# A hybrid decoder layer with expert retrieval: one output packed, the order around the first gathers changed, the chain spread wider, the end split over partitions

## The chip, the cores and the metric

The kernel runs on one core of one Trainium2 chip. The metric is the device time of one execution in microseconds (us); the time of a kernel is the median of several runs.

## The reference, cut to what matters

A prompt of 512 rows (four tiles of 128) and 8 sample rows, all of width 1024 in fp32, go through one layer:

```python
h = x + W_out(concat[A, B, C, D](rmsnorm(x) @ W_in))     # A: causal convolution over 31 rows, B: RWKV-7, C: gated convolution over 3 rows, D: pooling
q = rmsnorm(h) @ wq                                        # 8 heads of 256 columns
s1, s2 = q[:, :, 0] . k1, q[:, :, 1] . k2                  # 128 keys each
v1, i1 = top_k(s1, 16); v2, i2 = top_k(s2, 16)
sc, pos = top_k(v1[..., :, None] + v2[..., None, :], 16)   # 16 of the 256 sums, for each head
e = i1[pos // 16] * 128 + i2[pos % 16]; g = softmax(sc)    # 128 experts a row
y = rmsnorm(h + sum_s g_s * gelu(u_tab[e_s] . h2) * v_tab[e_s])
```

`h2` is the second normalised input, rmsnorm(h). The tables u and v have 16384 rows of 1024. The new states of A to D are outputs too; C's state of the samples (`shortconv_sample`) is one of them.

## The kernel before, in words

All work is laid out by hand on five engines, each with its own instruction stream, with semaphores between them. There are two phases.

**The mixers of tiles 0 and 1.** x is normalised, turned and multiplied with the 19 column blocks of W_in, first for the band of tiles 0, 1 and the samples, then for the band of tiles 2 and 3 (`zcol` on TensorE, `zc` the copy on ScalarE, 38 in all). The weights go through three buffers, `wring`, loaded by SyncE's queue in the order of `BLOCKS` (`weights(n)` waits until a buffer is free). The mixers of the first band run between the column blocks. Then `first_out` multiplies with the eight blocks of W_out for tiles 0 and 1; three blocks of tile 1 (`ASIDE`) have buffers of their own.

**The expert slots.** `UNITS` lists 32 units, each a head and a tile, and a last one for the samples. A prompt unit has 16 slots; the samples' unit has 8, since all their heads fit in one set of 64 partitions. Slots have a running number k from 0 to 519. For each slot GpSimd issues one gather of 128 rows of 8 KB (a row of u and of v side by side) into a ring of 8 rows (`RING`); VectorE makes the dot product with u (line 1877); ScalarE makes gelu, the weight and a diagonal matrix `diag` (lines 1301 to 1307); TensorE multiplies `diag` with v into PSUM (line 1000, samples line 992) and gives the ring row free (`slot_used`). Two units ahead of its use (`LEAD`), `query` and `score` (lines 923 and 932) and VectorE's `choose` find the experts of a unit. Its weights `wqk`, 1.125 MB a head in five pieces, are loaded by SyncE's queue in `next_keys` once the previous head's last product is done. Pass 1 (units 0 to 15) takes heads 0 to 7 over tiles 0 and 1, pass 2 (units 16 to 31) heads 0 to 7 over tiles 2 and 3.

**The chain in pass 1.** The RWKV mixer of tiles 2 and 3, their output product and second norm are cut into 162 steps (`mixer(1)`, a generator on each engine). `pace(k)` says up to which step an engine goes after slot k, so the order is fixed by a formula. Step 121 (`C_OUT`) starts the output product (line 634), 162 is the last copy. `W_SLOT` is the slot from which the eight W_out blocks for it are loaded.

**Where the streams meet.** Nothing in a stream passes what is ahead of it: a DMA on SyncE's queue waits for all those issued ahead on that queue, ScalarE's `queries(2)` stands ahead of `softmax(1)`, which unit 0's last step on VectorE waits for. A change of the function table on ScalarE is an instruction of its own (ACT_TABLE_LOAD): gelu, exp, sqrt and sigmoid lie in different tables; Square and Copy need no load of their own in any row of this trace.

## Time and profile before

| | before |
|---|---|
| median of 3 runs | 1711.93 us (1711.45 to 1715.87) |
| the profiled execution, its time / its span | 1719.7 us / 1717.8 us |
| TensorE busy | 1232.3 us (72%) |
| VectorE busy | 1243.2 us (72%) |
| ScalarE busy | 700.2 us (41%) |
| GpSimd busy | 907.9 us (53%) |
| bytes moved by DMA | 606.61 MB, of them 545.29 MB by the gathers |
| granted TensorE clock, mean | 0.841 of full speed |

All rows below are of the profiled execution; their times count from the start of its span. Its own time lies 0.5% above the median of the runs. A row of the timeline gives start, duration, engine, line and operation, what is written and read, how many instructions it merges, and in brackets how long the engine was idle before it and what ended the idle time. An fp32 matmul of the source is two instructions in the trace, so "x4" for a pair of matmuls is no mistake.

### The profile page before, as it was taken

The page shows a single profiled execution, that of the slowest core. Times are in us where ns is not written, and L with a number is a line of the kernel's source. Part 1 is how long each engine was busy: PE and PEld are TensorE (multiplying, and loading weights), DVE is VectorE, ACT ScalarE, POOL GpSimd, SP SyncE. Part 2 cuts the span into 40 slices and gives each one's busy share as a digit, 9 for nine tenths or more (in the row PEclk, how much of TensorE's full clock was granted, in tenths as well). Part 3 has the DMA queues.
Part 4 walks back from the last instruction along what each step waited for, and adds up shares of the span by engine and source line. Part 5 has one row for each costly group of instructions (what it writes and reads, how often), then busy time and mean ns, then how long its engine had stood idle before and what let it go on. Part 6 is the DMA issues. An engine that isn't in the chain of part 4 may idle for free.

```text
span 1717.8 us, 19398 instructions
## 1 busy us (share of the span) xinstructions
PE 1232.3 (72%) x5360; PEld 617.3 (36%) x5360; DVE 1243.2 (72%) x2955; ACT 700.2 (41%) x1988; POOL 907.9 (53%) x1134
## 2 busy tenths in 40 slices
PE   7998888466777777769966666666666666566555
PEld 5887746222344443324322323222222322222110
DVE  3868756589788877777786777677777677767775
ACT  3322115364434444334555444343434343334344
POOL 0264012355576565545665656565656555656662
PEclk9999999677889898868997868788778788877778
DMA  6321476699999999998999999999999999999996
GB/s 199 123 86 50 95 236 178 245 401 365 386 384 417 417 417 419 417 417 362 394 414 418 419 416 418 418 415 410 414 403 416 418 410 414 404 417 417 414 408 255
DMA packets 111932, 606.61 MB, mean 353 GB/s; under 512 B 24896, under 2 KB 27456, under 8 KB 45264
## 3 DMA queue, kind: packets, MB, share of 16 engines
q0 software_dynamic: 74880, 545.29, 78.2%
q1 hardware_dynamic: 36944, 60.09, 10.8%
q8 instruction: 42, 0.69, 0.2%
q14 instruction: 66, 0.54, 0.1%
HBM read 602.15 MB, written 3.19 MB: 352 GB/s over the span
## 4 chain that ended last, share of the span: by engine, by line
DMA 39%; PE 25%; DVE 13%; POOL 7%; issue 6%; ACT 5%; DVEq 3%; SPq 2%; POOLq 0%; ACTq 0%
DMA arena<-in_uv,arena 37%; PE ps L1000 9%; DVE arena L1877 6%; PE ps L583 5%; POOL arena L2108 4%; DVEq L1340 3%; POOL arena L2107 3%; DVE arena L1343 3%; PE ps L923 3%; PE ps L647 2%; PE ps L634 2%; SPq L510 2%; DVE arena L1349 1%; ACT arena L1307 1%; PE ps L627 1%
## 5 line engine op out<-in xcount | busy, mean ns | idle before, releaser
L1000 PE MATMUL ps<-arena 128*64 128x512 f32 x2048 | 659.3, 778 | 371.9 <-ACT arena L1307 371.6
L1877 DVE CUSTOM_DVE_ANT_0 arena<-arena 128x1024 f32<-128x1024 f32 x520 | 641.6, 1235 | 301.3 <-DMA arena<-in_uv,arena 284.0
L2108 POOL DMA_INDIRECT arena<-in_uv,arena x520 | 615.4, 1184 | 88.6 <-POOL arena L2107 18.6
L2107 POOL TENSOR_TENSOR arena<-arena 1x1 f32<-1x1 f32 x520 | 210.2, 404 | 547.7 <-PE ps L1000 403.0
L1000 PEld LDWEIGHTS ps<-arena 128*64 128x64 f32 x2048 | 151.1, 164 | 753.9 <-ACT arena L1307 517.8
L1301 ACT ACTIVATE arena<-arena 128x1 f32<-128x1 f32 x520 | 105.2, 202 | 735.1 <-DVE arena L1877 733.4
L1307 ACT ACTIVATE arena<-arena 128x64 f32<-128x64 f32 (+1 forms) x520 | 181.5, 349 | 16.9
L1303 ACT ACTIVATE arena<-arena 128x1 f32<-128x1 f32 x520 | 153.2, 295 | 16.9
L1343 DVE TENSOR_TENSOR arena<-arena 128x512 f32<-128x512 f32 (+6 forms) x310 | 133.5, 431 | 30.1 <-ACT arena L1047 16.8
L923 PE MATMUL ps<-arena 128*128 128x128 f32 x1024 | 129.1, 287 | 21.6 <-DMA arena<-in_wqk 20.5
L923 PEld LDWEIGHTS ps<-arena 128*128 128x128 f32 x1024 | 123.2, 200 | 58.0 <-issue 35.7
L583 PE MATMUL ps<-arena 128*128 128x264 f32 (+1 forms) x608 | 142.6, 391 | 0.4 <-DVE arena L1343 0.4
L583 PEld LDWEIGHTS ps<-arena 128*128 128x128 f32 x608 | 116.4, 194 | 21.7 <-issue 2.5
L1928 POOL TENSOR_TENSOR arena<-arena 128x512 f32<-128x512 f32 (+12 forms) x69 | 71.1, 1038 | 99.4 <-ACT arena L1047 43.0
L647 PE MATMUL ps<-arena 128*128 128x128 f32 x576 | 80.8, 293 | 37.8 <-ACT arena L1080 25.6
L1349 DVE SCALAR_TENSOR_TENSOR arena<-arena 128x256 f32<-128x256 f32 (+4 forms) x164 | 98.1, 636 | 6.3
L647 PEld LDWEIGHTS ps<-arena 128*128 128x128 f32 x576 | 73.8, 203 | 64.2 <-issue 33.2
L1346 DVE TENSOR_SCALAR arena<-arena 64x8 f32<-64x8 f32 (+6 forms) x244 | 62.4, 260 | 25.5 <-ACT arena L1021 8.7
L1047 ACT ACTIVATE arena<-ps 128x264 f32<-128x264 f32 (+1 forms) x38 | 14.8, 388 | 114.2 <-PE ps L583 114.2
L1301 ACT ACT_TABLE_LOAD x45 | 57.7, 1283 | 0.8
L1343 DVE TENSOR_TENSOR arena<-arena,ps 128x512 f32<-128x512 f32 (+3 forms) x50 | 38.3, 793 | 22.6 <-PE ps L589 9.3
L634 PE MATMUL ps<-arena 128*128 128x512 f32 (+1 forms) x96 | 44.6, 619 | 1.6 <-DVE arena L1343 1.3
(161 smaller groups left out, 950.6 us busy)
## 6 DMA issues: line engine op xcount, KB each, us to landing
arena<-in_win SPq DMA_DIRECT2D x38, 512.0 KB, 3.3
arena<-in_wqk SPq DMA_DIRECT2D x64, 256.0 KB, 7.7
arena<-in_wout SPq DMA_DIRECT2D x24, 512.0 KB, 7.4
arena<-in_uv,arena POOLq DMA_INDIRECT x520, 12.2
arena<-in_xp SPq DMA_DIRECT2D x4, 512.0 KB, 7.2
arena<-in_wqk SPq DMA_DIRECT2D x16, 128.0 KB, 9.4
out_yp<-arena SPq DMA_DIRECT2D x4, 512.0 KB
arena<-in_const SPq DMA_DIRECT2D x1, 864.0 KB, 8.9
```

What stands on the lines that cost most here:

```text
L583: last = mm(ps[:, j % 2, 0:hi - lo], wring[:, n % 3, k, :], hT[:, k, lo:hi], start=(k == 0), stop=(k == KT - 1))
L647: last = mm(ps[:, bank, 128 * j:128 * j + 128], left[:, 4 * q + j, :], right if right is ident else right[:, 4 * q + j, :], start=True, st ...
L923: last = mm(ps[:, 4, 128 * half:128 * half + 128], wq[:, k, 128 * half:128 * half + 128], hq[t][:, k, QOFF[t]:QOFF[t] + 128], start=(k == ...
L1000: last = mm(ps[64 * q:64 * q + 64, b + c, :], diag[:, (s + q) % 8, :], ring[:, (s + q) % RING, D + 512 * c:D + 512 * c + 512], start=(s == ...
L1301: f(gl[:, b, s:s + 1], hsel[:, b, s:s + 1], ACT.Gelu).then_inc(S["gelu_done"], 1)
L1303: f(wgt[:, b, s:s + 1], gl[:, b, s:s + 1], ACT.Copy, scale=gate[:, t, s:s + 1]).then_inc(S["weight_done"], 1)
L1307: f(diag[:, s % 8, 0:64 if u < NU else NS], imask if u < NU else cst("sel2"), ACT.Copy, scale=wgt[:, b, s:s + 1]).then_inc(S["diag_done"], 1)
L1343: return v.tensor_tensor(out, i0, i1, op)
L1349: return v.scalar_tensor_tensor(out=out, in0=i0, scalar=s, in1=i1, op0=op0, op1=op1)
L1877: v.tensor_tensor_reduce(out=ring[:, s % RING, 0:D], in0=ring[:, s % RING, 0:D], in1=row, scale=1.0, scalar=0.0, op0=MUL, op1=ADD, accum_o ...
L2107: pool.tensor_tensor(carrier[:, 1:2], carrier[:, 0:1], carrier[:, 0:1], ALU.add).then_inc(S["carried"], 1)
L2108: pool.indirect_dma_start(out=ring[:, s % RING, :], out_offset=None, in_=a["uv"][:, :], in_offset=bass.IndirectOffsetOnAxis(ap=idx[:, t, s ...
```

## The change

What it does, part by part:

- **Packed state output.** The new state of C for the samples leaves from a contiguous copy `ssc_out` (made by GpSimd) instead of from a strided view of `extq`; the wait of VectorE's chain on that transfer goes.
- **Start.** x is loaded ahead of the identity; the sqrt table is loaded ahead of all else on ScalarE; tile 0's square sum, root and norm are done without waiting for tile 1 and the samples.
- **hT split.** The turned input of the two bands lies in two places, so gather 4 waits only for the first band's column blocks, and gather 5 for all.
- **First output products.** Tile 1's blocks 1 to 3 are multiplied after `score(0)`, the aside blocks are loaded later on SyncE's queue, and the steps of the convolution's layernorm for tiles 2 and 3 move behind tile 0's second norm.
- **Unit 0.** `query(2)` stands after the products of slots 0 to 5, not of 0 and 1; `queries(2)` on ScalarE at slot 7, not 5.
- **Pace.** Two chain steps in three slots instead of three in four; `W_SLOT` 166 instead of 152. The last step stands at slot 251 instead of 224.
- **Pass 2** takes heads 7 to 0, so head 7's weights are not loaded again at its start; the samples' query of a head is made beside tile 3's unit, not tile 2's.
- **Samples.** Their output product alternates between two 64-column halves of the array (one more VectorE addition); their expert products put columns 0 to 511 on partitions 0 to 7 and 512 to 1023 on 32 to 39; the final norm works on 40 x 512 instead of 8 x 1024; the sqrt table is loaded right after the last `diag`; tile 3's final norm stands 2 to 4 slots earlier; two half transfers store the result, one on ScalarE's queue.

```diff
-UNITS = [(h, t) for h in range(FIRST) for t in (0, 1)] + [(h, t) for h in range(FIRST) for t in (2, 3)] \
-    + [(h, t) for h in range(FIRST, HEADS) for t in range(TILES)]
+UNITS = [(h, t) for h in range(FIRST) for t in (0, 1)] + [(h, t) for h in reversed(range(HEADS)) for t in (2, 3)]
...
-W_SLOT = 152
+W_SLOT = 166
...
-    return 3 * (k - START) // 4
+    return 2 * (k - START) // 3
...
-            sp_.dma_start(ident, a["const"][:, 0:128]).then_inc(d_ident, 16)
             sp_.dma_start(x[:, 0, :], a["xp"][0:128, :]).then_inc(d_x[0], 16)
             sp_.dma_start(x[:, 1, :], a["xp"][128:256, :]).then_inc(d_x[1], 16)
+            sp_.dma_start(ident, a["const"][:, 0:128]).then_inc(d_ident, 16)
...
-                if n == n_out + 9:
-                    sp_.wait_ge(S["short_done"], 2)
-                    for i, j in enumerate(ASIDE):
-                        sp_.dma_start(w_aside[i], a["wout"][:, OUT_ORDER[j], :]).then_inc(d_aside, 16)
+                elif 5 <= k < 5 + len(ASIDE):
+                    if k == 5:
+                        sp_.wait_ge(S["short_done"], 2)
+                    sp_.dma_start(w_aside[k - 5], a["wout"][:, OUT_ORDER[ASIDE[k - 5]], :]).then_inc(d_aside, 16)
...
-            sp_.dma_start(a["o_ssc"][:, :, :, :], extq[:, :, :, 1:SK]).then_inc(d_ssc, 16)
+            sp_.dma_start(a["o_ssc"][:, :, :, :], ssc_out).then_inc(d_ssc, 16)
...
+            def project_samples(nh):
+                y = Y_ROWS[TILES][1]
+                for j in range(KT):
+                    p = 64 * (j % 2)
+                    last = mm(ps[p:p + NS, 5 + nh, :], y[:, OUT_ORDER[j], :], w_blocks[j][:, 512 * nh:512 * nh + 512], start=(j < 2), stop=(j >= KT - 2))
...
-            first_out(1, 0, 2)
+            first_out(1, 0, 1)
             conf_mean(1)
-            first_out(1, 2, 4)
-            conf_variance(1)
             turned(0, 0)
             turned(0, 1)
...
             query(0)
+            conf_variance(1)
             score(0)
-            first_out(1, 4, 8)
+            first_out(1, 1, 8)
...
-                if s == 0:
+                late = 4 if v == LEAD else 0
+                if s == late:
                     query(v)
-                elif s == 6:
+                elif s == (9 if late else 6):
                     score(v)
...
-                            last = mm(ps[0:NS, b + c, :], diag[:, s, 0:NS], ring[:, s % RING, D + 512 * c:D + 512 * c + 512],
+                            last = mm(ps[HALVES[c], b, :], diag[:, s, 0:NS], ring[:, s % RING, D + 512 * c:D + 512 * c + 512],
...
-            for part in (XORDER[:3], XORDER[3:]):
+            act.wait_ge(S["eps_set"], 1)
+            f(st[:, 3, 0:1], eps[:, 0:1], ACT.Sqrt)
+            for part in (XORDER[:1], XORDER[1:2], XORDER[2:3], XORDER[3:]):
...
-            final_squares(TILES)
-            final_root(TILES)
+            f(graw[:, 0:1], eps[:, 0:1], ACT.Sqrt)
+            act.wait_ge(S["unit_added"], TILES + 1)
+            f(sq2s[BOTH], xs2[BOTH], ACT.Square, accum_out=st[BOTH, 0, TILES:TILES + 1]).then_inc(S["fin_sq"], 1)
...
                     elif k == 4:
+                        pool.wait_ge(S["z_copied"], NZ)
+                    elif k == 5:
                         pool.wait_ge(S["z_copied"], len(ZORDER))
```

SyncE's queue before and after the packed output; the first row is the output of the tails, `in_lora` the small weights for the chain, `in_wqk` head 1's query weights. Before:

```order
L507 DMA out_o_tails<-arena 128x94 [waits tails_done]
L508 DMA out_o_ssc<-arena 2048x1x2
L510 DMA arena<-in_lora 128x256 [waits d_swkv]
L521 DMA arena<-in_wqk 128x512 [waits q_mm]
L521 DMA arena<-in_wqk 128x512 x3
```

After:

```order
L515 DMA out_o_tails<-arena 128x94 [waits tails_done]
L516 DMA out_o_ssc<-arena 128x32
L518 DMA arena<-in_lora 128x256 [waits d_swkv]
L529 DMA arena<-in_wqk 128x512 [waits q_mm]
L529 DMA arena<-in_wqk 128x512 x3
```

The order is the same; the state output has 128 rows of 32 values where it had 2048 pieces of 2.

TensorE from the output products of tile 1 to unit 0's slots. Before (583 is `zcol`, 589 the convolution's layernorm, 627 `first_out`, 641 `turned`, 923 and 932 query and score, 1000 the slots):

```order
L627 MATMUL ps<-arena 128x512 x4
L589 MATMUL ps<-arena 128x256 x2
L641 MATMUL ps<-arena 128x128 x8
L923 MATMUL ps<-arena 128x128 x16
L932 MATMUL ps<-arena 128x128 x2
L627 MATMUL ps<-arena 128x512 x8
L583 MATMUL ps<-arena 128x256 x32
L641 MATMUL ps<-arena 128x128 x8
L583 MATMUL ps<-arena 128x256 x8
L923 MATMUL ps<-arena 128x128 x16
L932 MATMUL ps<-arena 128x128 x2
L1000 MATMUL ps<-arena 64x512 x4
```

After (591 is `zcol`, 597 the layernorm, 635 `first_out`, 657 `turned`, 940 and 949 query and score, 1018 the slots):

```order
L597 MATMUL ps<-arena 128x256 x2
L657 MATMUL ps<-arena 128x128 x8
L940 MATMUL ps<-arena 128x128 x16
L597 MATMUL ps<-arena 128x256 x2
L949 MATMUL ps<-arena 128x128 x2
L635 MATMUL ps<-arena 128x512 x14
L591 MATMUL ps<-arena 128x256 x32
L657 MATMUL ps<-arena 128x128 x8
L591 MATMUL ps<-arena 128x256 x8
L940 MATMUL ps<-arena 128x128 x16
L949 MATMUL ps<-arena 128x128 x2
L1018 MATMUL ps<-arena 64x512 x12
```

`turned` and `query` of unit 0 have moved ahead of six matmuls of `first_out`, which now stand in one piece of 14 behind the first score; slots 0 to 5 (12 rows) stand ahead of the third query, where it was slots 0 and 1 (4 rows).

ScalarE at its end. Before (1026 is a root, 1301 to 1307 a slot's gelu, weight and diag, 1269 the final squares):

```order
L1026 ACT_TABLE_LOAD
L1026 ACTIVATE arena<-arena 128x1
L1301 ACT_TABLE_LOAD
L1301 ACTIVATE arena<-arena 128x1
L1303 ACTIVATE arena<-arena 128x1
L1307 ACTIVATE arena<-arena 128x8
L1269 ACTIVATE arena<-arena 8x1024
L1026 ACT_TABLE_LOAD
L1026 ACTIVATE arena<-arena 8x1
```

After (1320 to 1326 a slot, 1342 the table's early load, 1344 and 1346 the samples' squares and root):

```order
L1320 ACTIVATE arena<-arena 128x1
L1322 ACTIVATE arena<-arena 128x1
L1326 ACTIVATE arena<-arena 128x8
L1342 ACT_TABLE_LOAD
L1342 ACTIVATE arena<-arena 128x1
L1344 ACTIVATE arena<-arena 40x512
L1346 ACTIVATE arena<-arena 40x1
L1348 DMA out_ys<-arena 8x512
L212 UNCONDITIONAL_BRANCH
```

The root of tile 3 with its two table loads no longer stands ahead of the last slot's gelu, and the table for the samples' root is loaded ahead of the squares.

## Rows read from the trace of the kernel before

**Rows 1.** Windows: stretch, length, busy by engine, PEclk, DMA share, GB/s.

```profile
325.00:493.00 168.00, 112.14 (x476) 48.55 (x474) 134.83 (x321) 86.15 (x231) 101.01 (x124) 0.80 0.94 370
...
606.00:732.00 126.00, 95.14 (x468) 47.78 (x468) 96.22 (x245) 52.51 (x166) 72.91 (x96) 0.87 1.01 417
732.00:877.00 145.00, 119.62 (x422) 46.25 (x422) 109.02 (x259) 65.50 (x180) 77.80 (x96) 0.86 0.97 395
...
1002.00:1604.00 602.00, 401.47 (x1668) 163.53 (x1668) 431.52 (x1098) 246.50 (x776) 363.35 (x457) 0.80 1.01 413
```

**Rows 2.** SyncE's queue in time: start, us, transfer.

```profile
276.13 0.55 SPq L508 DMA_DIRECT2D out_o_ssc<-arena  x1
276.73 27.18 SPq L510 DMA_DIRECT2D arena<-in_lora  x1
303.95 9.57 SPq L521 DMA_DIRECT2D arena<-in_wqk  x4
```

**Rows 3.** DMA issues by line: count, KB each, us to landing.

```profile
arena<-in_win SPq DMA_DIRECT2D x38, 512.0 KB, 3.3
arena<-in_wqk SPq DMA_DIRECT2D x64, 256.0 KB, 7.7
...
arena<-in_uv,arena POOLq DMA_INDIRECT x520, 12.2
...
arena<-in_ssc SPq DMA_DIRECT2D x1, 16.0 KB, 3.9
out_o_ssc<-arena SPq DMA_DIRECT2D x1, 16.0 KB, 42.6
```

**Rows 4.** TensorE's timeline, 234 to 328 us.

```profile
234.68 3.66 PE L627 MATMUL ps<-arena 128*128 128x512 f32 x8
243.05 6.28 PE L627 MATMUL ps<-arena 128*128 128x512 f32 x8 [4.71 <-DMA arena<-in_wout]
...
256.41 3.81 PE L923 MATMUL ps<-arena 128*128 128x128 f32 x32 [1.04 <-DVE arena L1421]
...
287.40 3.73 PE L923 MATMUL ps<-arena 128*128 128x128 f32 x32
...
321.07 6.55 PE L923 MATMUL ps<-arena 128*128 128x128 f32 x32 [20.52 <-DMA arena<-in_wqk]
```

**Rows 5.** GpSimd's timeline, 275 to 331 us.

```profile
275.64 1.14 POOL L2108 DMA_INDIRECT arena<-in_uv,arena  x1 [0.17 <-issue]
...
329.57 0.18 POOL L2107 TENSOR_TENSOR arena<-arena 1x1 f32<-1x1 f32 x1 [25.66 <-PE ps L1000]
```

**Rows 6.** VectorE's timeline, 300 to 335 us.

```profile
305.22 1.23 DVE L1877 CUSTOM_DVE_ANT_0 arena<-arena 128x1024 f32<-128x1024 f32 x1 [1.63 <-DMA arena<-in_uv,arena]
...
331.39 0.16 DVE L1831 RECIPROCAL arena<-arena 128x1 f32<-128x1 f32 x1 [15.31 <-ACT arena L1263]
...
334.06 1.23 DVE L1877 CUSTOM_DVE_ANT_0 arena<-arena 128x1024 f32<-128x1024 f32 x1
```

**Rows 7.** Timeline at the start: ScalarE, then TensorE.

```profile
8.68 1.28 ACT L1026 ACT_TABLE_LOAD   x1
...
16.95 17.48 PE L583 MATMUL ps<-arena 128*128 128x264 f32 x64 [0.36 <-DVE arena L1343]
```

**Rows 8.** TensorE's timeline, 844 to 853 us.

```profile
844.31 7.04 PE L634 MATMUL ps<-arena 128*8 128x512 f32 x16
851.28 1.94 PE L1000 MATMUL ps<-arena 128*64 128x512 f32 x8
```

**Rows 9.** Timeline at the end: ScalarE, TensorE, VectorE.

```profile
1705.93 1.28 ACT L1301 ACT_TABLE_LOAD   x1
...
1712.48 1.28 ACT L1026 ACT_TABLE_LOAD   x1
...
1708.15 1.89 PE L992 MATMUL ps<-arena 128*8 128x512 f32 x4 [1.80 <-ACT arena L1307]
...
1714.23 1.27 DVE L1349 SCALAR_TENSOR_TENSOR arena<-arena 8x1024 f32<-8x1024 f32 x1
```

154 lines of the change are left out of this document (98 added, 56 removed).

## The prediction

> **What bounds the kernel now.** I read the windows first. From 1002 to 1604 us the DMA engines are busy throughout at 413 GB/s while TensorE and VectorE work two thirds of the time: pass 2 is the gathers' stream, and a gather of 1.049 MB costs 2.54 us there [rows 1]. Nothing that only shortens an engine's work helps in it. The same is true from 606 to 732, at 417. Two stretches move less: 325 to 493 (370 GB/s, with VectorE at 134.8 of 168 us) and 732 to 877 (395, with TensorE at 119.6 of 145) [rows 1]. At 417 GB/s they would be 168 x (1 - 370/417) = 18.9 and 145 x (1 - 395/417) = 7.6 us shorter.
>
> Then I read the queues ahead of that, because a stream that starts late ends late. TensorE stands 20.52 us ahead of the third query, waiting for head 1's `wqk` [rows 4]. SyncE's queue says why it is late: behind the state output, issued at 276.13, the small `in_lora` load occupies the queue for 27.18 us, and head 1's weights are issued only from 303.95 [rows 2]. The state output needs 42.6 us to land although it has 16 KB [rows 3]. Its 2048 pieces of 8 bytes are 128 for each of 16 DMA engines, so one piece takes 42.6/128 = 0.33 us. A gather's 8 KB row takes 8192 B over 413/16 GB/s = 0.32 us. I read it as the engines alternating between the two queues, one piece for one row. The load of the same state, also 2048 pieces, landed in 3.9 us with no gathers about [rows 3]. Meanwhile GpSimd waits 25.66 us to 329.57 for a free ring row, so the DMA engines run dry too [rows 5], and VectorE stands 15.31 us at unit 0's last choosing step, which waits for ScalarE's softmax behind `queries(2)` [rows 6].
>
> **The change part by part.**
>
> *Start, -4.* The table load at 8.68 (1.28 us) stands between the third square sum and the first root; the column blocks begin at 16.95 [rows 7]. Now the load is done before x lands, and tile 0 does not wait for two more tiles. Walking the same durations forward, the first turn starts at 7.4, the samples' is done at 12.6, the blocks start at 13.0. TensorE is near full in what follows, so 4 us stay. Bounds: 2, if the small inputs (their issue is not earlier) hold the mixer, and 4.5.
> The Trainium skill (ScalarE: Activation LUTs, What ACT_TABLE_LOAD costs) puts a table switch at 2.66 us, drain included. The row after the load here starts 1.3 us behind it, so the trace does not agree; by the page the three loads that leave the path (one here, two at the end) would give 4 us more than my sum.
>
> *Order up to the second query, -5.* TensorE idles 4.71 us at 243.05 for a W_out block that lies behind three aside blocks on the queue, the eight matmuls behind it take 6.28 instead of 3.66, and 1.04 are lost ahead of `query(0)` [rows 4]: 8.3 in sum. The asides are later now. But `turned(0)` now follows one block and waits for the second norm, about 3 us. 8.3 - 3 = 5: `query(1)` ends near 282 instead of 291.1, the start's 4 included. Bounds: 0, if the last column blocks of W_in, now loaded beside the first gathers, are late (3.3 us to land alone, a key piece beside gathers 7.7 [rows 3]), and 8.3. `score(0)` comes some 15 us earlier, so gather 0 is issued near 258 instead of 275.64 [rows 5]. I cost that at nothing: the ring holds 8 rows and the first product still waits for the last column block. The hT split likewise lets one more gather go ahead of that block; also nothing.
>
> *The queue, -15.* With 128 rows of 128 bytes there are 8 pieces an engine, and `in_lora` and the keys go at once. Head 1's weights are issued when `query(1)` is done and land in about 8 us [rows 3], before slots 0 to 5, now ahead of `query(2)`, are through. What limits then is VectorE, whose nine dot products and the choosing of unit 1 run to the dot of slot 8 as they did. So the 15.31 us go, and the 1.63 of waiting for a gather at 305.22 [rows 6]; the softmax with its table load still costs some 2. The dot of slot 9, 334.06 before, comes at 334.1 - 4 - 5 - 15 = 310. Bounds: 9, if the keys are still late by half; and more than 15, since gather 10, issued right after 329.57, could go near 294: up to 26 if VectorE did not limit.
>
> *Pace, units 0 to 3, -4.* Each slot carries 0.67 chain steps for 0.75. Of VectorE's 134.8 us, 54 dots of 1.23 and their read-out take 70 [rows 6]; choosing and chain share 65, and a ninth of the chain's part is some 3 us; waits on the chain's round trips go with it. Bounds 0 and 8.
>
> *Pace and halves, units 9 to 12, -5.* An output product holds TensorE for 7.04 us, and its samples' two are two of six [rows 8]. Spread over 10.5 slots for 9.3, with the samples' two at half, TensorE is asked for less than the gathers take. Of 7.6 us (above) I take 5; bounds 1 and 7.6. The halving is from the row behind: eight matmuls in two halves of the array take 1.94, where 16 without take 7.04, 3.5 for eight [rows 8].
> The chain now ends at slot 251 of 256. `query(16)` stands at slot 224, its input at step 143, VectorE's slot 223: just in time, at no cost, since VectorE runs a slot or two ahead of TensorE.
>
> *Head 7 kept, -2.5.* 1.18 MB at 413 GB/s are 2.9 us of a full stream; I take 2.5.
>
> *End, -4.* The load at 1705.93 ahead of the last gelu goes to an earlier slot: 1.2 [rows 9]. The one at 1712.48 is done under the last product: 1.28. Three steps over 8 x 1024 (VectorE's last of 1.27 [rows 9], its addition and ScalarE's squares, which I take as alike) become 40 x 512 and halve: 1.7. The last slot's product of 1.89 [rows 9] may halve as above: up to 0.9. Two small additions and drains cost 0.5. Between 3.7 and 4.6 in sum; I take 4, bounds 2.5 and 5.
>
> **Sum.** 4 + 5 + 15 + 4 + 5 + 2.5 + 4 = 39.5. The profiled execution, 1719.7, would be 1680.2; the median of the runs lies 7.8 below it, so 1711.9 - 39.5 = 1672.4.
>
> **The rivals.**
> *The queue stays slow.* 128-byte rows are still small, and if it is the gathers and not the pieces that hold SyncE's queue, head 1's weights are late again and only 24.5 us come back: 1687. Against it: key pieces of 2 KB rows land beside gathers in 7.7 us [rows 3].
> The Trainium skill (DMA: Bandwidth & Descriptors, Specifications) asks for at least 512 B a transfer for line rate, which 128 B does not reach; that rule speaks for this rival, and no row here has 128 B rows beside gathers.
> *The gathers alone bound it.* If VectorE is not the limit once the stop is gone, 512 gathers from 289 on at 2.54 us (1300), 14 key loads at 2.9 (40), the W_out blocks (10), some 5 to land and 9 to finish give a span of 1653, in the median near 1647; half of that way is 1659.
> *Slower.* The last W_in blocks are loaded while gathers 0 to 4 hold the DMA engines. Each block's buffer is freed by the one before it, so their delays add up. At a gather's landing of 12.2 us for 3.3 each [rows 3], five blocks would cost 44 us, more than all gains: 1716. It decides from 8.5 us late a block. Against it: only two or three are issued after gather 0, and key pieces need 7.7.
> *Nothing moves.* Only if the stop were made up later; but the stretches at 413 to 417 GB/s have no room to make up anything.
>
> **How the numbers follow.** Forecast, 1660 to 1680: 0.62. Queue stays slow, 1680 to 1692: 0.15. Towards the gathers' bound, 1647 to 1660: 0.18. Slower: 0.02; within 0.3% (about what a measurement of this kernel tells from no change): 0.01; between, 1692 to 1707: 0.02. The range 1655 to 1690 leaves 0.1 below and 0.1 above. Faster by over 0.3%: 0.97.
>
> **What would show it.** The column blocks start near 13 us. Gather 0 near 258, `query(1)` done near 282. The state output lands in under 10 us and `in_lora` holds the queue under 2. No wait over 5 us ahead of the third query, VectorE's dot of slot 9 near 310. The stretch from there to unit 4 moves near 380 GB/s, that of the output products over 405. From the start of the last product to the end under 7.5 us, for 9.65 now (1708.15 to the span's 1717.8). I am wrong if VectorE or ScalarE stands for over 10 us anywhere between 260 and 330, or if unit 16 starts with a wait for its rows.

## The result and the profile after

| | before | changed |
|---|---|---|
| median of the runs on the same chip | 1713.90 us (4 runs) | 1692.99 us (4 runs, 1692.44 to 1696.31) |
| ratio to before | | 0.9881, 95% 0.9861 to 0.9900 |
| span of the profiled execution | 1717.8 us | 1690.7 us (its own time 1692.44) |
| granted TensorE clock, mean | 0.841 | 0.847 |

The change makes the kernel faster by 20.9 us in the medians, where the forecast was 39.5. Two later measurements of the same kernel on other chips gave 0.9859 (0.9829 to 0.9889) and 0.9860 (0.9835 to 0.9885), 24.6 and 25.2 us. The two traces shown side by side differ by 27.1 us; the trace of before is one of its longer executions.

The page of the changed kernel, the row on DMA: packets, bytes, and small packets.

```profile
DMA packets 109308, 605.43 MB, mean 358 GB/s; under 512 B 22904, under 2 KB 25336, under 8 KB 42640
```

605.43 MB for 606.61: one head's keys less, as the change says.

The windows of the changed kernel, stages as in [rows 1], then two short ones at the end: stretch, length, busy by engine, PEclk, DMA share, GB/s.

```profile
306.00:467.50 161.50, 107.76 (x460) 48.15 (x460) 133.83 (x328) 87.39 (x230) 95.69 (x116) 0.79 0.97 379
704.00:862.00 158.00, 119.64 (x448) 50.07 (x450) 113.91 (x281) 63.38 (x189) 85.11 (x107) 0.85 0.98 395
816.00:862.00 46.00, 42.86 (x156) 17.73 (x154) 32.84 (x81) 20.60 (x58) 27.43 (x34) 0.96 0.89 344
978.00:1579.50 601.50, 400.86 (x1662) 166.27 (x1664) 430.31 (x1093) 247.22 (x773) 354.77 (x456) 0.80 1.01 414
1664.00:1670.00 6.00, 3.10 (x12) 0.34 (x12) 3.47 (x7) 4.06 (x10) 2.98 (x4) 0.99 1.03 430
1679.00:1686.00 7.00, 3.77 (x8) 0.22 (x8) 1.92 (x3) 3.30 (x9) 0.00 (x0) 0.50 0.01 5
```

The stretch from the third query to unit 4 moves 379 GB/s for 370 (380 was forecast). The stretch with the output products stays at 395 (over 405 was forecast), and in its last third it falls to 344, with TensorE busy in 42.86 of 46 us. Pass 2 is the same stream: 414 for 413.

The start of the changed kernel in the timeline (against [rows 7]).

```profile
13.23 1.06 ACT L1039 ACTIVATE arena<-arena 128x1024 f32<-128x1024 f32 x1 [3.97 <-DMA arena<-in_xp]
...
15.69 0.15 DVE L1370 TENSOR_SCALAR arena<-arena 128x1 f32<-128x1 f32 x1 [1.12 <-ACT arena L1039]
15.76 0.21 DVE L1367 TENSOR_TENSOR arena<-ps,arena 128x64 f32<-128x64 f32 x1
...
16.03 15.96 PE L591 MATMUL ps<-arena 128*128 128x264 f32 x64 [3.32 <-DVE arena L1367]
```

The column blocks start at 16.03, not at 13. TensorE waits 3.32 us for VectorE's step on the samples' turned rows (15.76), and VectorE has just done a mean at 15.69, of the last tile: its square sum follows the one at 13.23, which waited 3.97 us for x. The samples stand in VectorE's order behind the means of tiles 2 and 3.

SyncE's queue (against [rows 2]), and the landing of the state output (against [rows 3]).

```profile
248.47 0.43 SPq L512 DMA_DIRECT2D arena<-in_wout  x1
...
250.19 0.44 SPq L512 DMA_DIRECT2D arena<-in_wout  x1
251.54 19.81 SPq L471 DMA_DIRECT2D arena<-in_win  x4
...
271.86 0.43 SPq L516 DMA_DIRECT2D out_o_ssc<-arena  x1
272.34 0.43 SPq L518 DMA_DIRECT2D arena<-in_lora  x1
288.35 2.04 SPq L529 DMA_DIRECT2D arena<-in_wqk  x4
```

```profile
out_o_ssc<-arena SPq DMA_DIRECT2D x1, 16.0 KB, 7.3
```

The state output lands in 7.3 us, `in_lora` occupies the queue for 0.43 us where it was 27.18, and head 1's keys are issued at 288.35, 15.6 us earlier than in [rows 2].

ScalarE's last copy of a second-band column block ahead of the first score, TensorE between 251 and 310 us, and GpSimd's gathers (against [rows 4, 5]).

```profile
231.15 0.39 ACT L1067 ACTIVATE arena<-ps 128x256 f32<-128x256 f32 x1 [10.77 <-PE ps L591]
...
251.93 1.99 PE L635 MATMUL ps<-arena 128*128 128x512 f32 x4 [0.42 <-DMA arena<-in_wout]
256.94 7.12 PE L635 MATMUL ps<-arena 128*128 128x512 f32 x12 [3.02 <-DMA arena<-in_wout]
...
275.60 3.73 PE L591 MATMUL ps<-arena 128*128 128x256 f32 x16 [1.15 <-DMA arena<-in_win]
...
284.59 3.73 PE L940 MATMUL ps<-arena 128*128 128x128 f32 x32
...
306.04 3.84 PE L940 MATMUL ps<-arena 128*128 128x128 f32 x32
...
258.61 1.14 POOL L2164 DMA_INDIRECT arena<-in_uv,arena  x1 [0.17 <-issue]
...
285.25 0.18 POOL L2163 TENSOR_TENSOR arena<-arena 1x1 f32<-1x1 f32 x1 [20.04 <-ACT arena L1067]
```

The wait of 20.52 us ahead of the third query is gone. Gather 0 goes at 258.61, as forecast. But `query(1)` starts at 284.59 and ends at 288.3, not at 282. TensorE waits 0.42 and 3.02 us for `in_wout`, pays 7.12 us for twelve matmuls behind the second wait (the granted clock is 0.79 from 256 to 264 us; in a later trace, at 1.00, the twelve take 5.43), and waits 1.15 us for `in_win` at 275.60. The queue shows why. The three aside blocks are issued one at a time between the ring's blocks; the last goes at 250.19 and lands at 256.89, where TensorE's second wait ends. The row of `in_win` merges four issues of 0.33 us each, between which SyncE waits for free buffers. Two of them, at 267.55 and 271.02, go behind gathers 0 to 4 and take 8.01 and 7.72 us to land, where the last two of before took 3.15 and 3.67; TensorE's wait at 275.60 is for the first of these. GpSimd then waits 20.04 us, so the early gathers bring no early stream.

Of the two signs of being wrong that the prediction named, the first comes up at its edge: ScalarE stands 13.01 us, until 267.56, for a column block that comes behind the run of output products; 7.6 us of that lie behind 260. VectorE stands nowhere over 6 us there. The second does not come up: unit 16's first dot waits 0.20 us, and the 2.10 us that VectorE waits for `in_nf` just ahead of it fall where the DMA share is 1.01.

VectorE in the changed kernel: the softmax's reciprocal in unit 0, the dot of slot 9, and the first dots of units 4, 9 and 13 (against [rows 6]); then the latter three in the kernel before.

```profile
312.05 0.16 DVE L1856 RECIPROCAL arena<-arena 128x1 f32<-128x1 f32 x1 [0.86 <-ACT arena L1282]
...
314.75 1.23 DVE L1928 CUSTOM_DVE_ANT_0 arena<-arena 128x1024 f32<-128x1024 f32 x1
...
467.49 1.23 DVE L1928 CUSTOM_DVE_ANT_0 arena<-arena 128x1024 f32<-128x1024 f32 x1 [0.18 <-issue]
...
677.00 1.23 DVE L1928 CUSTOM_DVE_ANT_0 arena<-arena 128x1024 f32<-128x1024 f32 x1 [0.18 <-DMA arena<-in_uv,arena]
...
861.78 1.23 DVE L1928 CUSTOM_DVE_ANT_0 arena<-arena 128x1024 f32<-128x1024 f32 x1 [0.73 <-DMA arena<-in_uv,arena]
```

```profile
493.56 1.22 DVE L1877 CUSTOM_DVE_ANT_0 arena<-arena 128x1024 f32<-128x1024 f32 x1
...
701.47 1.23 DVE L1877 CUSTOM_DVE_ANT_0 arena<-arena 128x1024 f32<-128x1024 f32 x1 [0.20 <-issue]
...
884.43 1.23 DVE L1877 CUSTOM_DVE_ANT_0 arena<-arena 128x1024 f32<-128x1024 f32 x1
```

The stop of 15.31 us is 0.86 now. From slot 9 to unit 4 it is 152.7 us for 159.5, to unit 9 209.5 for 207.9, and from there to unit 13 184.8 for 183.0 (in a second trace of each, 182.3 for 185.3; both scatter).

The end of the changed kernel: SyncE's two stores of `yp`, TensorE, the last two dots, and the table load (against [rows 9]). Then the last dot and the two stores of before.

```profile
1660.34 12.48 SPq L555 DMA_DIRECT2D out_yp<-arena  x2
...
1665.79 1.03 PE L1010 MATMUL ps<-arena 128*8 128x512 f32 x4 [0.43 <-ACT arena L1326]
...
1683.16 1.88 PE L1010 MATMUL ps<-arena 128*8 128x512 f32 x4 [1.32 <-ACT arena L1326]
...
1677.76 1.23 DVE L1928 CUSTOM_DVE_ANT_0 arena<-arena 128x1024 f32<-128x1024 f32 x1 [1.74 <-DMA arena<-in_uv,arena]
...
1680.96 1.23 DVE L1928 CUSTOM_DVE_ANT_0 arena<-arena 128x1024 f32<-128x1024 f32 x1 [1.97 <-DMA arena<-in_uv,arena]
...
1683.12 1.28 ACT L1342 ACT_TABLE_LOAD   x1
```

```profile
1704.76 1.23 DVE L1877 CUSTOM_DVE_ANT_0 arena<-arena 128x1024 f32<-128x1024 f32 x1 [1.25 <-DMA arena<-in_uv,arena]
...
1685.35 22.49 SPq L547 DMA_DIRECT2D out_yp<-arena  x2
```

From the last dot to the end it is 9.7 us for 13.0; from the last product's start 7.5 for 9.65. The table load at 1683.12 lies under the product, as planned. Two rows are not as planned. The last product takes 1.88 us, though the same four matmuls in two halves take 1.03 at 1665.79: the windows show a granted clock of 0.99 there and 0.50 (1.2 GHz) at the end, where TensorE had stood idle between its products for up to 2.67 us; before, the window from 1706 to 1711 us has 1.00. And the last two dots wait 1.74 and 1.97 us for gathers, where the last of before waits 1.25.

### The profile page after: what moved, and what is told of

It reads as the page before. It is cut to its first block, busy times and chain, and to the rows that moved or that the text cites. A ratio compares the mean times of both kernels' runs of the same rounds, so it can differ in the third digit from the quotient of the medians.

```text
span 1690.7 us, 19411 instructions
## 1 busy us (share of the span) xinstructions
PE 1217.4 (72%) x5360; PEld 611.3 (36%) x5360; DVE 1249.3 (74%) x2965; ACT 703.5 (42%) x1990; POOL 903.2 (53%) x1135
## 2 busy tenths in 40 slices
DMA packets 109308, 605.43 MB, mean 358 GB/s; under 512 B 22904, under 2 KB 25336, under 8 KB 42640
## 4 chain that ended last, share of the span: by engine, by line
DMA 39%; PE 24%; DVE 17%; POOL 6%; issue 5%; ACT 4%; DVEq 4%; SPq 0%; POOLq 0%
DMA arena<-in_uv,arena 37%; PE ps L1018 10%; DVE arena L1928 9%; PE ps L591 5%; POOL arena L2164 4%; DVEq L1364 4%; DVE arena L1367 3%; PE ps L940 2%; POOL arena L2163 2%; PE ps L663 2%; DVE arena L1373 1%; ACT arena L1326 1%; ACT arena L1322 1%; PE ps L635 1%; DVE arena L1370 1%
## 5 line engine op out<-in xcount | busy, mean ns | idle before, releaser
L2163 POOL TENSOR_TENSOR arena<-arena 1x1 f32<-1x1 f32 x520 | 204.2, 393 | 530.8 <-PE ps L1018 430.4
L1367 DVE TENSOR_TENSOR arena<-arena 64x8 uint32<-64x8 f32 (+8 forms) x312 | 134.7, 433 | 23.8 <-ACT arena L1067 15.3
L940 PEld LDWEIGHTS ps<-arena 128*128 128x128 f32 x1024 | 122.1, 198 | 36.0 <-issue 35.9
L940 PE MATMUL ps<-arena 128*128 128x128 f32 x1024 | 128.0, 285 | 1.0 <-DVE arena L1449 1.0
L591 PEld LDWEIGHTS ps<-arena 128*128 128x128 f32 x608 | 114.3, 191 | 25.9 <-DVE arena L1367 3.4
L663 PE MATMUL ps<-arena 128*128 128x128 f32 x576 | 77.7, 288 | 19.9 <-ACT arena L1100 9.3
L663 PEld LDWEIGHTS ps<-arena 128*128 128x128 f32 x576 | 71.5, 199 | 44.2 <-issue 22.6
L1367 DVE TENSOR_TENSOR arena<-arena,ps 128x512 f32<-128x512 f32 (+4 forms) x51 | 39.0, 791 | 16.3 <-PE ps L635 6.8
L1928 DVE DVE_READ_ACCUMULATOR2_ANT arena<- 128x1 f32 x520 | 43.0, 83 | 0.0
```

The costliest lines, as they stand in the source:

```text
L591: last = mm(ps[:, j % 2, 0:hi - lo], wring[:, n % 3, k, :], hT[g][:, k, :], start=(k == 0), stop=(k == KT - 1))
L663: last = mm(ps[:, bank, 128 * j:128 * j + 128], left[:, 4 * q + j, :], right if right is ident else right[:, 4 * q + j, :], start=True, st ...
L940: last = mm(ps[:, 4, 128 * half:128 * half + 128], wq[:, k, 128 * half:128 * half + 128], hq[t][:, k, QOFF[t]:QOFF[t] + 128], start=(k == ...
L1367: return v.tensor_tensor(out, i0, i1, op)
L1928: v.tensor_tensor_reduce(out=ring[:, s % RING, 0:D], in0=ring[:, s % RING, 0:D], in1=row, scale=1.0, scalar=0.0, op0=MUL, op1=ADD, accum_o ...
L2163: pool.tensor_tensor(carrier[:, 1:2], carrier[:, 0:1], carrier[:, 0:1], ALU.add).then_inc(S["carried"], 1)
```

## The experiments

All are timed on chips beside the kernel before; "ratio" is to it, with its 95% interval. Since front phases differ between executions of one program, traces are compared by stretches: A, from ScalarE's copy at 231.15 (its like in each kernel) to `query(1)` done; B, from there to the dot of slot 9; and from slot 9 on. Units are bounded by their first dots.

**The kernel before once more.**

> The kernel before, unchanged, for a second trace. The changed kernel's span is 27.1 us shorter than the first trace's, but the medians differ by 20.9. If the first trace was a slow execution, this one ends near 1711 and the 6 us are missing evenly over the gathers' stream, or in one place; if the trace itself costs time, it is near 1718 again, and so should the changed kernel's have been.

Measured: span 1719.4 us, one time of 1721.26 beside a median of 1715.85. A is 53.7 us (56.2 in the first trace), B 45.5 (42.9). So A scatters by 2.5 us in one program.

**The changed kernel once more,** twice, on the chips of later experiments.

> The changed kernel, unchanged, beside the three runs below. Four traces of kernels with the same program up to the second query end that query at 293.9 to 295.8, the changed kernel's first trace at 288.3. If that trace was a lucky one, this one ends near 294 and its span is near 1697; ratio to before 0.987 to 0.989.

Measured: 1694.18 us, 0.9859 (0.9829 to 0.9889).

> The changed kernel once more, unchanged, on the chip of the three kernels beside it, so that they are compared with it and not only with the kernel before. Expected: 1693 us, 0.986 of before. In its trace query(1) ends between 288 and 296 (288.3 and 293.4 in its two traces so far), since that end scatters between executions of one program.

Measured: 1696.24 us, 0.9860 (0.9835 to 0.9885). A is 58.2 and 58.6 us (57.2 in the first trace); `query(1)` ends at 293.5 and 291.6. From slot 9 to the end, the three traces have 1375.9, 1373.7 and 1377.8.

**The packed output alone.**

```diff
-            sp_.dma_start(a["o_ssc"][:, :, :, :], extq[:, :, :, 1:SK]).then_inc(d_ssc, 16)
+            sp_.dma_start(a["o_ssc"][:, :, :, :], ssc_out).then_inc(d_ssc, 16)
...
-                    dve.wait_ge(d_ssc, 16)
...
+                link(pool.tensor_copy(ssc_out, extq[:, :, :, 1:SK]))
```

> The kernel before with the packed state output alone. By the theory that the 2048 pieces hold SyncE's queue, in_lora no longer occupies the queue for 27 us, the 15 us stand of VectorE goes, and the time falls by 15 to 18 us: ratio 0.990. By the rival (gathers hold the queue whatever the pieces) under 5 us. If the ratio is 0.988 or less, this part alone is the whole gain of the change and all else adds up to nothing.

Measured: 1700.65 us, 0.9913 (0.9892 to 0.9935), 15.2 us less than before. B is 29.3 us for 42.9 and 45.5. This one edit is two thirds of the whole gain and as large as forecast. VectorE's wait for the transfer, which it also takes out, held nothing: in the kernel before the transfer had landed at 318.74, and VectorE stood until 331.39 for ScalarE.

What the 2048 pieces did can be read from the DMA packets of the kernel before, here from 290 to 314 us: queue, packets, MB, share of the 16 engines; the gathers' queue, then SyncE's.

```profile
q0 software_dynamic: 1122, 8.17, 92.5%
q1 hardware_dynamic: 1259, 0.38, 6.5%
```

Among these packets 998 gather rows of 8 KB and 986 pieces of 8 bytes start, one piece for one row, as the prediction had read it from the totals; in the second trace of before it is 891 rows and 1002 pieces. A piece by itself takes 9 ns, and from 280 to 282 us 779 of them went through. So it was the waiting for its turn behind a row that cost 0.33 us a piece. In the second trace the output took 45.3 us and `in_lora` occupied the queue for 28.7.

The timeline of the kernel with the packed output alone, TensorE's third query, ScalarE's copy of its result and VectorE's reciprocal, shows what is late next.

```profile
303.75 5.79 PE L924 MATMUL ps<-arena 128*128 128x128 f32 x32 [7.62 <-DMA arena<-in_wqk]
...
309.58 0.39 ACT L1252 ACTIVATE arena<-ps 128x256 f32<-128x256 f32 x1 [8.46 <-PE ps L924]
...
313.31 0.16 DVE L1831 RECIPROCAL arena<-arena 128x1 f32<-128x1 f32 x1 [3.74 <-ACT arena L1264]
```

The third query waits 7.62 us for head 1's keys, ScalarE stands behind it for 8.46, and VectorE 3.74 behind ScalarE's softmax; in the changed kernel that last wait is 0.86.

**The pace as before.**

```diff
-W_SLOT = 166
+W_SLOT = 152
...
-    return 2 * (k - START) // 3
+    return 3 * (k - START) // 4
```

> The changed kernel with the old pace and the old slot for the W_out loads. By the predicted terms (4 us in units 0 to 3, 5 in units 9 to 12) it is 9 us slower than the changed kernel, ratio to before 0.993. By the traces the slower pace gave some 5 us in units 0 to 3 and lost 2 in units 9 to 12: 3 us slower, 0.990. Rival: the pace moves only where the time is spent, and the two are equal, 0.988.

Measured: 1694.86 us, 0.9875 (0.9855 to 0.9895). From slot 9 to unit 4 it is 160.5 us (152.7 changed), from unit 9 to 13 183.1 (182.3 to 184.8), from slot 9 to the end 1380.7, where nine traces with the slower pace (and pass 2 from head 7 down) have 1373.2 to 1377.8. The pace is worth 7 to 8 us in units 0 to 3 (all four traces with the old pace have 158.4 to 160.5 there) and gives some of it back later. Net it is some 5 us in the traces, but with the old pace and the changed rest this is one trace, of its slowest execution (1703.29 us), and the medians don't resolve it.

**Pass 2 with heads 0 to 7.**

```diff
-UNITS = [(h, t) for h in range(FIRST) for t in (0, 1)] + [(h, t) for h in reversed(range(HEADS)) for t in (2, 3)]
+UNITS = [(h, t) for h in range(FIRST) for t in (0, 1)] + [(h, t) for h in range(HEADS) for t in (2, 3)]
...
-                h = HEADS - 1 - n
+                h = n
```

> The changed kernel with heads 0 to 7 in pass 2, so head 0's weights are loaded again after head 7's (1.18 MB more). By the predicted term it is 2.5 us slower (ratio to before 0.990). The trace shows no gain between units 15 and 17, by which it is equal (0.988), and the stream has room for one load there.

Measured: 1697.55 us, 0.9885 (0.9866 to 0.9904). From unit 13 to the end it is 829.7 us, where the three traces of the changed kernel have 828.9, 830.0 and 829.3: under 1 us, too little to tell.

**Aside loads together; then gather 0 held until the last but three column blocks are done.**

```diff
-                elif 5 <= k < 5 + len(ASIDE):
-                    if k == 5:
-                        sp_.wait_ge(S["short_done"], 2)
-                    sp_.dma_start(w_aside[k - 5], a["wout"][:, OUT_ORDER[ASIDE[k - 5]], :]).then_inc(d_aside, 16)
+                elif k == 5:
+                    sp_.wait_ge(S["short_done"], 2)
+                    for i, j in enumerate(ASIDE):
+                        sp_.dma_start(w_aside[i], a["wout"][:, OUT_ORDER[j], :]).then_inc(d_aside, 16)
...
+                    if k == 0:
+                        pool.wait_ge(S["z_done"], len(ZORDER) - 3)
```

> The changed kernel with the three aside blocks loaded together at 237 us, into a queue that is empty until 248 in the trace. By the theory that the order's 5 us were lost to late loads, TensorE's waits of 0.4 and 3.0 ahead of the aside blocks go, its matmuls behind them run at full clock (some 2 us), and the second query ends 5 us earlier; total 4 to 5 us faster than the changed kernel, ratio to before 0.985. Rival: VectorE's choosing of unit 0 or ScalarE's copies take over, under 1.5 us.

Measured: 1691.13 us, 0.9838 (0.9808 to 0.9867); A is 54.9 us.

> The same, and gather 0 held back until the third last column block is done, so that the last W_in loads meet no gathers. If gathers 0 to 4 delay those loads (wait of 1.15 us, in_win 8 us to land), another 1 to 3 us are won over the run before it; if gather 0's early issue was worth something, it is slower by up to 5 us.

Measured: 1686.70 us, 0.9812 (0.9788 to 0.9837); A is 52.7 us. The timeline of the second one: TensorE's last column blocks and `query(1)`, GpSimd's gather 0.

```profile
264.08 14.03 PE L591 MATMUL ps<-arena 128*128 128x256 f32 x64
...
283.35 3.73 PE L940 MATMUL ps<-arena 128*128 128x128 f32 x32
...
272.12 1.14 POOL L2166 DMA_INDIRECT arena<-in_uv,arena  x1 [0.63 <-issue]
```

The 64 matmuls run in one piece, without the wait for `in_win`. Gather 0 goes 13.5 us later than in the changed kernel and B is 26.6 us, as there (26.4). The last two W_in blocks land in 3.28 and 3.44 us, for 8.01 and 7.72: the early gathers only delayed W_in.

**A part of the output products left out.** This kernel leaves 6 of the 8 blocks of the output product out for tiles 2 and 3, and 4 of 8 for the samples.

```diff
-                for j in range(KT):
+                for j in (0, KT - 1):
```

> The changed kernel with two of eight blocks (four of eight for the samples) in the output products of tiles 2, 3 and the samples; the other products are left out, so h of these tiles lacks most of the mixers' part. It prices TensorE's blocks of 7 us in units 10 to 13. By the theory that they, standing in one piece in TensorE's order, let the ring run dry, the stretch at 344 GB/s returns to over 405 and the time falls by 6 to 9 us (ratio 0.983). If the chain's other steps or the W_out loads are what costs, under 2 us.

Measured: 1691.13 us, 0.9849 (0.9823 to 0.9875). Units 9 to 12 take 180.5 us, where ten traces with the same pace and the product in full have 182.3 to 184.8, 183.7 in the mean: 3.2 us for some 20 us of TensorE's time taken away (the four pieces of the prompt tiles take 28.4 us in the changed kernel and 8.8 here). All that the part left out still costs the stream is some 3 us.

**Three speeds.**

```diff
-W_SLOT = 166
+W_SLOT = 154
...
-    return 2 * (k - START) // 3
+    if k < 76:
+        return 2 * (k - START) // 3
+    if k < 170:
+        return 45 + 4 * (k - 76) // 5
+    return 120 + (k - 170) // 2
```

> The changed kernel with a pace of three speeds: 2 steps in 3 slots to slot 76, 4 in 5 to slot 170, 1 in 2 behind it, so that the output products stand 6 to 8 slots apart instead of 4.5 to 6. If TensorE's demand in that stretch is the cost, 4 to 6 us faster than the changed kernel (0.985). If each block of 7 us costs by itself because it is longer than the ring's lead, little changes: under 1.5 us.

Measured: 1697.12 us, 0.9872 (0.9847 to 0.9898); units 9 to 12 take 186.3 us. Spreading them further this way does not help, but the first product here waits 5.72 us for `in_wout`, where it waits 0.28 before and not at all in the changed kernel, so the run doesn't separate wider spacing from late weights.

**The samples' features ahead of the means of tiles 2 and 3.**

```diff
+            features(TILES)
...
-            features(TILES)
```

> The changed kernel with VectorE's hT step of the samples ahead of the two means of tiles 2 and 3. In the changed kernel's trace this step starts at 15.76, behind the mean of tile 3 that waits for x of tile 3, and TensorE idles 3.3 us ahead of the first column block. By this theory the idle time goes, the blocks start at 12.7 to 13.5 and 2.5 to 3.5 us are won: 0.986. Rival: the first W_in block has not landed by then (the DMA engines are full until 15 us), and under 1 us is won.

Measured: 1691.07 us, 0.9842 (0.9812 to 0.9872), 3.1 us less than the changed kernel beside it; its executions lie at 1688.13 to 1693.02, those of the changed kernel at 1693.01 to 1696.99. TensorE in its timeline:

```profile
12.74 10.99 PE L591 MATMUL ps<-arena 128*128 128x264 f32 x48 [0.60 <-DVE arena L1367]
```

The column blocks start at 12.74, as the forecast's walk of the start had it.

**Output products in halves of 3.6 us.**

```diff
-            def project_out(t, nh):
+            def project_out(t, nh, lo, hi):
...
-                for j in range(KT):
+                for j in range(lo, hi):
...
+                    yield C_OUT + 7 * k + 2
+                    project(k, 0, 1)
```

> The changed kernel with each 7 us output product of tiles 2 and 3 cut into two of 3.5 us with slots between. If a block costs time because it is longer than what eight ring rows can bridge, units 9 to 12 (184 us from dot 144 to dot 208) get 3 to 6 us shorter, near 179, as with the products cut out (180.5). If TensorE's total demand is the cost, nothing changes, since the work is the same.

Measured: 1690.19 us, 0.9843 (0.9812 to 0.9874); units 9 to 12 take 180.8 us, and 180.4 to 181.9 in the three later kernels with the halves, 181.2 in the mean, against 183.7 above: 2.5 us, nearly as much as leaving most of the product out. TensorE's timeline, first of the changed kernel, then with the halves:

```profile
807.63 7.14 PE L642 MATMUL ps<-arena 128*128 128x512 f32 x16
```

```profile
807.28 3.72 PE L642 MATMUL ps<-arena 128*128 128x512 f32 x8
...
817.12 3.70 PE L642 MATMUL ps<-arena 128*128 128x512 f32 x8
```

Behind the block of 7.14 us the products of two slots follow in one piece; behind one of 3.7 us it is one slot's. By unit, both gains lie in unit 12, where three of the four blocks of the changed kernel stand (827.92, 838.47, 851.63): 43.2 to 45.7 us in the ten traces, 41.4 with the products cut, 41.3 to 42.8 in halves. Two limits of this reading: from 816 to 858 us of the kernel with the halves TensorE is busy for 42.00 of 42 us, so there is no room for more; and the packed output alone, with the old pace and whole blocks, has units 9 to 12 in 180.1 us too, so the gain of the halves is shown at the slower pace alone.

**All four together** (features first, aside loads together, gather 0 held, halves).

> The changed kernel with the samples' hT step first, the asides loaded together, gather 0 held back for the last W_in loads, and the output products cut in two. If the four causes add up (3, 4.5, 2 and 4 us), the second query ends near 284, the stream follows, and the ratio to before is 0.980; with nothing from the first and the last it is 0.983.

Measured: 1680.76 us, 0.9783 (0.9752 to 0.9814), beside 1694.18 for the changed kernel and 1718.76 for before. It beats both.

**The old order of first products, layernorm steps and aside loads.**

```diff
-            first_out(1, 0, 1)
+            first_out(1, 0, 2)
             conf_mean(1)
+            first_out(1, 2, 4)
+            conf_variance(1)
...
-            conf_variance(1)
             score(0)
-            first_out(1, 1, 8)
+            first_out(1, 4, 8)
```

> The changed kernel with one part undone: the order of the first output products, of the convolution's layernorm steps and of the aside loads is that of before, all else as changed. Theory: that part cost 3 to 6 us where I forecast a gain of 5, through the waits for W_out and W_in blocks on SyncE's queue and the slow matmuls behind them. Then query(1) ends at 54 to 56 us behind the second band's first z copies (57 to 61 in the traces of the changed order, 54 to 56 in those of before), near 285 to 290, and the median is 1688 to 1690. Rival: the order is worth what I forecast (5 us) and the later end in the traces is scatter; then the median is near 1698, and query(1) ends past 296. Second rival: the order is worth nothing either way, and the median is within 2 us of the changed kernel's.

Measured: 1692.09 us, 0.9840 (0.9816 to 0.9863), 4.1 us less than the changed kernel beside it (1696.24). The copy that starts A, and TensorE:

```profile
235.17 0.39 ACT L1068 ACTIVATE arena<-ps 128x256 f32<-128x256 f32 x1 [10.82 <-PE ps L591]
...
241.93 5.21 PE L635 MATMUL ps<-arena 128*128 128x512 f32 x8 [3.35 <-DMA arena<-in_wout]
...
265.99 14.03 PE L591 MATMUL ps<-arena 128*128 128x256 f32 x64
...
285.27 3.73 PE L942 MATMUL ps<-arena 128*128 128x128 f32 x32
```

A is 285.27 + 3.73 - 235.17 = 53.8 us, for 57.2, 58.2 and 58.6. The wait for `in_wout` at 241.93 is back, but the column blocks run in one piece from 265.99. The intervals of the two ratios overlap, but trace and median point the same way and to the same size, and the traces don't overlap: eleven with the changed order and the aside loads one at a time have A at 56.5 to 61.1 us, the four with the old order at 53.7 to 56.2.

**The third query back at slot 0.**

```diff
-                late = 4 if v == LEAD else 0
+                late = 0
...
-                    if s == (7 if u == 0 else 5) and u + LEAD < NU:
+                    if s == 5 and u + LEAD < NU:
```

> The changed kernel with the third query back at slot 0 of unit 0 and queries(2) at slot 5, as before. Theory: the query stood later for a wait that the packed output removes anyway; its place costs about 2.8 us between query(1) and the dot of slot 9 or nothing: in the trace the third query then waits for head 1's weights for some 8 us, slots 0 to 5 behind it come late by as much, but the dot of slot 9 comes 1 to 3 us later than 26.4 us behind query(1) (29.3 in the kernel with the packed output alone). Expected median 1694 to 1697, 0.987 of before. Rival: the move is worth nothing, and the 2.8 us are scatter between two executions; then 1693 and 26 to 27 us.

Measured: 1694.43 us, 0.9852 (0.9831 to 0.9872); B is 25.4 us, so the place is worth nothing. But the wait is not the 8 us that I expected; TensorE:

```profile
305.05 6.70 PE L940 MATMUL ps<-arena 128*128 128x128 f32 x32 [2.40 <-DMA arena<-in_wqk]
```

It is 2.40 us, for 7.62 with the packed output alone. In that kernel four gathers are issued around the keys' issue (283.97 to 287.89, keys from 286.73), here three (to 293.12, keys from 293.27), the fifth having gone early.

**Gather 4 waits for the last column block.**

```diff
-                        pool.wait_ge(S["z_copied"], NZ)
-                    elif k == 5:
                         pool.wait_ge(S["z_copied"], len(ZORDER))
```

> The changed kernel with one wait of the gathers' queue as before: gather 4 waits for the last column block of W_in, as all later ones do, so the split of the turned input brings nothing. Between query(1) and the dot of slot 9 the changed kernel takes 25.4 to 26.7 us, with the old order and with the third query at its old place too, where before with the packed output alone takes 29.3. Theory: these 2.8 us are the fifth gather that goes ahead of the last column block, 2.54 us of a full stream. Then it is 28 to 30 us here and the median is 2 to 3 us above the changed kernel's, near 1697. Rival: the extra gather buys nothing, and the 2.8 us come from another part (the chain's slower pace in unit 0); then 26 to 27 us and a median near 1694.

Measured: 1695.67 us, 0.9882 (0.9855 to 0.9908); B is 26.7 us. VectorE's reciprocal at 311.48 has waited 1.11 us for ScalarE, near the 0.86 of the changed kernel, so my theory falls. The late query and the extra early gather each suffice to take the keys' lateness off the softmax, and each was taken back with the other in place. Both taken back together was not run.

**The samples' preparations one unit earlier, and spread over four slots.** Both start from the best kernel.

```diff
-                    if u == NU - 1 and s >= 13:
+                    if u == NU - 2 and s >= 13:
```

> The best kernel so far (features ahead of the means, aside loads together, gather 0 held, output products in halves) with VectorE's copies of the samples' indices and weights (split_samples) one unit earlier. Theory: these copies in the last prompt unit are the 1.2 us by which the stretch from unit 30's first dot to the last dot is longer in all kernels with the changed end (101.5 for 100.3). Then that stretch is 100.3 here and the median 1 us lower, 1679.5. Rival: the copies cost nothing there; the 1.2 us are the samples' query, which now stands beside tile 3's unit instead of tile 2's. Then the stretch stays at 101.5 and the median at 1681.

Measured: 1681.94 us, 0.9784 (0.9760 to 0.9807); from unit 30 to the last dot 101.7 us.

```diff
-                    if u == NU - 1 and s >= 13:
-                        split_samples(s - 13)
+                    if u == NU - 1 and s in (10, 12, 13, 14):
+                        split_samples((10, 12, 13, 14).index(s))
```

> The best kernel so far with VectorE's preparations of the samples' end (two pairs of copies of 0.41 us each and the memsets) spread over slots 10, 12, 13 and 14 of the last prompt unit, where they stood in slots 13 to 15, the four copies together with tile 3's last addition of 1.30 us in slot 15. Theory: one late dot in slot 15 (4.40 us behind the last for 2.81 before) frees ring rows late and the last gathers go later; spread, each piece fits into the 1.2 us that VectorE waits for a gather anyway, the unit takes 40.1 us again for 41.7, and the whole end from unit 30's first dot to the last is 100.3 for 101.5. Median 1679.5. Rival: what counts is the sum and not the piece (one unit earlier it was 101.7); then 101.5 and 1681.

Measured: 1682.34 us, 0.9800 (0.9778 to 0.9823); 101.5 us. The dot behind the last of these copies:

```profile
1646.64 1.23 DVE L1932 CUSTOM_DVE_ANT_0 arena<-arena 128x1024 f32<-128x1024 f32 x1 [1.34 <-DMA arena<-in_uv,arena]
```

It waits for a gather, not for VectorE. The whole stretch keeps its 101.5 us wherever the copies stand, so neither theory on them holds. What the rows of the end show instead: SyncE's two stores of `yp` are issued within 12.48 us from 1660.34, so the second, tile 3's 512 KB, goes at 1672.5, ahead of the last gathers' landing; before, it went at 1707.5, behind the last dot. At 413 GB/s it is 1.3 us of the stream, and the last two dots stand 2.97 and 3.20 us behind the one ahead, for 2.49 and 2.49 before: 1.2 us. This was read from the traces, not tried.

## Why the prediction missed

The direction and most mechanisms were right; the sum was not. By term, in us saved:

| term | forecast | measured | from |
|---|---|---|---|
| start | 4 | 1 | 16.03 for 16.95; the missing 3 come with features first |
| order up to the second query | 5 | -4 | the old order: A 3.4 to 4.8 shorter, median 4.1 less |
| queue | 15 | 15, and 3 with what stands around it | packed output alone; B 29.3, then 26.4 |
| pace, units 0 to 3 | 4 | 7 | 152.7 for 159.5; 160.5 with the old pace |
| units 4 to 8 | 0 | -1.5 | 209.5 for 207.9 |
| pace and halves, units 9 to 12 | 5 | -1 to 1 | 182.3 to 184.8; 180.1 to 185.3 with the old pace |
| head 7 kept | 2.5 | 0 to 1 | heads forward |
| end | 4 | 2 | 3.3 less 1.2 |
| sum | 39.5 | 21.5 to 24.5 | medians: 20.9, 24.6, 25.2 |

**The order, 9 of the 17 us missed.** The failed step is "8.3 - 3 = 5": it priced the removed waits and not the loads that replace them. The prediction named the danger under "Slower" (W_in blocks beside gathers 0 to 4) and set it aside because key pieces need 7.7 us. As it said, only two are issued behind gather 0; each takes 4 to 5 us longer to land than before, and the price is 1.15 to 1.8 us at `in_win` in the three traces. The larger part is upstream: the aside blocks, issued singly between the ring's blocks, arrive for a run of twelve matmuls that now stands in one piece. That gather 0 comes earlier (17 us by the rows) was costed at nothing, and that was right for the gain and wrong for the loss: held back, it gives 2 us (A 52.7 for 54.9).

**Units 9 to 12, 4 to 6 us.** The step took "of 7.6 us I take 5" from the difference between 417 and 395 GB/s, as if a lower demand on TensorE were all. With most of the product left out the stretch gives only 3.2 us, and with the product complete but in halves 2.5. So at this pace most of what the products cost is the length of one piece, not the sum, and the slower pace left each of the four pieces for tiles 2 and 3 at 7.0 to 7.1 us, three of them in unit 12. The samples' two did halve, to 3.61 each, and moved to 874.83 and 886.46, behind this stretch, where before had all six products in it: with less to do, the stretch got no shorter.

**The start, 3 us.** The walk of durations was right, its order was not: it let the samples' step go ahead of the means of tiles 2 and 3, which stand ahead of it on VectorE and wait for x. The bounds, 2 to 4.5, did not hold 1.

**The end, 2 us.** The table loads and half-size steps came in (9.7 for 13.0). The halved last product brought nothing, since it ran at half the granted clock, and tile 3's store moved into the gathers' stream.

**Head 7.** 2.9 us of a full stream were taken; at most 1 came back.

**What held.** The queue, by mechanism and size: one output of 2048 pieces held back everything behind it on SyncE, and 15 us are 15 us. The Trainium skill (DMA: Bandwidth & Descriptors, Specifications) asks for at least 512 B a transfer for line rate. No run here shows that rate for 128 B rows: these 16 KB land in 7.3 us, and in 3.7 to 11.6 over all traces with the packed output, and nothing waits for them. The rival "the queue stays slow" gave 1687, nearer to the result than the forecast, for a reason that the queue's rows refute. Pace in units 0 to 3 was mis-sized: 7 for 4. And 39.5 was a sum of seven terms as if they stood alone, with no term for what one part takes from another.

## What to carry to other kernels

When steps are moved, price the loads that they now meet, on each queue, before the waits that they leave; and walk the engine's own order, not the order of the data. One output in thousands of small pieces can hold a queue for tens of us: look for the one-row entry with a long time. Where a stream of short slots shares an engine with long blocks, cut the block before slowing its pace.

## What the runs showed of the hardware

- One program's front phase scatters: the changed kernel's `query(1)` ended at 288.3, 293.5 and 291.6 us in three executions. Windows show part of it: from 180 to 235 us the granted clock was 1.00, 0.94 and 1.00, and from 0 to 20 us 1.00, 1.00 and 0.85. A term under 3 us there needs paired medians.
- At the end of the changed kernel TensorE's products are 1.03 us at a granted clock of 0.99; after three of them, with 0.43 and 2.10 us idle between and 2.67 us behind them, the clock is 0.50 and each takes 1.88 us. Before, products of 1.89 us with 0.59 to 1.80 us idle between them kept 1.00. All 17 traces with the changed end have 1.88 or 1.89 us for the last product: halving a sparse piece of work gave back nothing.
- 2048 pieces of 8 bytes took 42.6 us beside gathers [rows 3], since the DMA engines took about one piece for one gather row (986 for 998 in 24 us) though a piece lasts 9 ns; 128 rows of 128 bytes of the same data took 7.3 us.
